# Encoder layer: the first stage rebuilt around column halves of x and pairs of weight units

## The reference, cut to what matters

```python
def rmsnorm(x, w):
    y = xf * lax.rsqrt(jnp.mean(xf * xf, axis=-1, keepdims=True) + EPS)
    return (y * w)
def swiglu(x, w_gate, w_up, w_down):
    return (silu(x @ w_gate) * (x @ w_up)) @ w_down
```

## Time and profile before

| what | value |
| --- | --- |
| median of three runs | 1214.18 us (1213.52 to 1215.35) |
| span of the profiled execution | 1213.9 us |
| TensorE matmul busy | 1125.2 us, 93% of the span |
| VectorE, ScalarE, GpSimd busy | 586.6, 319.1 and 460.9 us |
| mean granted TensorE clock | 0.953 |
| first matmul of the first feed-forward, start | 26.33 us |
| first matmul of unit 4, start | 52.73 us |

### The profile page before, as it was taken

One profiled execution on the slowest core, in us unless ns is written; L12 is line 12 of the kernel. 1 busy time (PEld: TensorE's weight loads), 2 busy tenths in 40 slices (PEclk: granted clock), 3 DMA queues, 4 the chain that ended last, 5 costly groups with the idle time before them and its releaser, 6 DMA issues.

```text
span 1213.9 us, 13708 instructions
## 1 busy us (share of the span) xinstructions
PE 1125.2 (93%) x5167; PEld 912.8 (75%) x5167; DVE 586.6 (48%) x774; ACT 319.1 (26%) x458; POOL 460.9 (38%) x211
## 2 busy tenths in 40 slices
PE   4999999999999799898899699879999999999996
PEld 3788888888887578787788356757888888888884
DVE  5584455441000747575664654546754455520004
ACT  4322222222222332111111643334222222222211
POOL 4554444444444542131222220255544444444420
PEclk9999999999999789898899788988999999999996
DMA  7133333323332422121112000130433333233301
GB/s 213 43 115 103 88 102 91 99 88 94 96 95 61 155 87 70 36 53 36 52 36 69 18 1 1 35 104 21 119 99 91 102 88 103 80 96 96 95 15 69
DMA packets 173628, 94.51 MB, mean 78 GB/s; under 512 B 11477, under 2 KB 169753, under 8 KB 173465
## 3 DMA queue, kind: packets, MB, share of 16 engines
q1 hardware_dynamic: 173168, 93.93, 26.2%
q10 hardware_dynamic: 424, 0.10, 0.0%
HBM read 91.92 MB, written 2.10 MB: 77 GB/s over the span
## 4 chain that ended last, share of the span: by engine, by line
PE 85%; DVE 9%; issue 2%; POOL 2%; ACT 1%; DMA 1%; SPq 0%; DVEq 0%; POOLq 0%; ACTq 0%
PE ps L612 23%; PE ps L613 23%; PE ps L614 23%; PE ps L745 4%; PE ps L853 2%; PE ps L709 1%; PE ps L710 1%; PE ps L711 1%; PE ps L783 1%; DVE xT L979 1%; PE ps L868 1%; POOL SSX L354 1%; DMA raw<-ffn_w_gate 1%; PE ps L816 1%; DVE TMP L978 1%
## 5 line engine op out<-in xcount | busy, mean ns | idle before, releaser
L341 POOL TENSOR_TENSOR WL<-raw,WH 128x1024 fp32r<-128x1024 f32 x168 | 407.1, 2426 | 682.6 <-ACT WH L402 682.6
L612 PE MATMUL ps<-XH,WH 128*128 128x512 f32 x912 | 369.1, 405 | 18.3 <-DVE XL L958 8.3
L613 PE MATMUL ps<-XL,WH 128*128 128x512 f32 x912 | 361.9, 397 | 0.0
L614 PE MATMUL ps<-XH,WL 128*128 128x512 f32 x912 | 361.0, 396 | 0.0
L402 ACT ACTIVATE WH<-raw 128x1024 fp32r<-128x1024 f32 (+1 forms) x170 | 176.1, 1038 | 594.5 <-PE ps L614 551.7
L612 PEld LDWEIGHTS ps<-XH,WH 128*128 128x128 f32 x912 | 175.0, 192 | 58.8 <-DVE XL L958 10.6
L614 PEld LDWEIGHTS ps<-XH,WL 128*128 128x128 f32 x912 | 174.4, 191 | 40.4
L613 PEld LDWEIGHTS ps<-XL,WH 128*128 128x128 f32 x912 | 175.1, 192 | 35.6
L612 PE MATMUL ps<-hh,WH 128*128 128x512 f32 x352 | 138.3, 393 | 0.0
L613 PE MATMUL ps<-hl,WH 128*128 128x512 f32 x352 | 137.6, 391 | 0.0
L614 PE MATMUL ps<-hh,WL 128*128 128x512 f32 x352 | 137.3, 390 | 0.0
(11 more groups left out here) (146 smaller groups left out, 937.4 us busy)
## 6 DMA issues: line engine op xcount, KB each, us to landing
raw<-ffn_w_gate SPq DMA_DIRECT2D x44, 512.0 KB, 3.8
raw<-ffn_w_up SPq DMA_DIRECT2D x44, 512.0 KB, 3.8
raw<-ffn_w_down SPq DMA_DIRECT2D x32, 448.0 KB, 3.3
raw<-w_in SPq DMA_DIRECT2D x22, 512.0 KB, 3.8
raw<-ffn_w_down SPq DMA_DIRECT2D x16, 512.0 KB, 3.6
raw<-w_out SPq DMA_DIRECT2D x8, 512.0 KB, 3.5
xin<-x SPq DMA_DIRECT2D x4, 512.0 KB, 5.5
raw<-w_in SPq DMA_DIRECT2D x8, 256.0 KB, 3.4
```

The source lines that it names most:

```text
L341: pool.tensor_tensor(WL[:, s, 0:size], raw[:, s, 0:size], WH[:, s, 0:size].bitcast(fp32), ALU.subtract).then_inc(lo_done, 3 if n == 2 else 1)
L612: nc.tensor.matmul(dst, WH[:, s, w], xh, start=first, stop=False)
L613: nc.tensor.matmul(dst, WH[:, s, w], xl, start=False, stop=False)
L614: return nc.tensor.matmul(dst, WL[:, s, w], xh, start=False, stop=last)
```

## The change

- x is loaded in halves by channel. The first half (channels 0 to 511 of all tokens, two transfers) comes before units 0 and 1, the second half between units 1 and 2. Each half has one semaphore.
- The first norm's weights have a semaphore of their own (`pre_in`), are transposed first, and are copied to `g0`.
- There are four `turn` banks. k = 0 to 3 are transposed at the start; k = 4 to 7 inside the first pair of units, after k = 1, 2, 3 and 4. Each of these waits until the bank's old block was copied to `xT`.
- XH and XL are made from the `turn` bank in PSUM, not from `xT`, which is now copied four blocks later (the last four after all low parts).
- Units 0 and 1 are multiplied first, through all k, then units 2 and 3. Between them TensorE waits for the copies of all of x and for the small loads, and transposes the small loads.
- The squares are taken by ScalarE along the rows of the untransposed x, with the row sum as an accumulated output; eight such sums (two halves by four token blocks) replace squares, GpSimd's sums and `stat`. `spread` comes after k = 3 of the second pair.
- ScalarE makes the high parts of units 0 to 3 between those of x (after k = 1, 2, 4, 5). Its sqrt is no longer preloaded: the order is sqrt, exp, sigmoid.

```diff
+        g0, ssx = sb("g0", [P, KD]), sb("ssx", [P, 3, TT])
...
-        turn = (ps[4], ps[5], ps[7])
+        turn = (ps[4], ps[5], ps[2], ps[3])
...
-        const_in, mix_in, x_in = sem("const_in"), sem("mix_in"), [sem(f"x_in{c}") for c in range(TT)]
-        CONST_IN, MIX_IN = 11 * 16, 4 * 16
+        const_in, mix_in, x_in = sem("const_in"), sem("mix_in"), [sem(f"x_in{h}") for h in range(2)]
+        CONST_IN, MIX_IN = 10 * 16, 4 * 16
...
+            def load_x(half):
+
+                f = slice(half * (D // 2), (half + 1) * (D // 2))
+                for c in range(0, TT, 2):
+                    src = io["x"][0, c * P:(c + 2) * P, f].rearrange("(c p) d -> p c d", p=P)
+                    sp.dma_start(xin[:, c:c + 2, f], src).then_inc(x_in[half], 16)
...
                 for b in range(NSLOT):
                     load(first + b, 0, (gate, up)[b % 2][:, :, (b // 2) * P:(b // 2 + 1) * P])
+                    if s == 1 and b == 1:
+                        load_x(1)
...
             sp.dma_start(ident[:, :], io["t_square"][:, 0:P]).then_inc(ident_in, 16)
-            for c in range(TT):
-                sp.dma_start(xin[:, c, :], io["x"][0, c * P:(c + 1) * P, :]).then_inc(x_in[c], 16)
+            load_x(0)
             load_ffn(1, FFN1)
...
                     lo(first + b, 0, SLOT)
-                sum_x(e)
+                if e:
...
-                act.wait_ge(stat_ready, s + 1)
-                nc.scalar.activation(rt_root[:, s, :], STAT[:, 0:TT], ACT.Sqrt, bias=eps[:, :], scale=1.0 / D).then_inc(root_ready, 1)
+                if s:
+                    act.wait_ge(stat_ready, s)
+                else:
+                    act.wait_ge(rows_summed, 1)
+                nc.scalar.activation(rt_root[:, s, :], STAT[:, 0:TT] if s else ssx[:, 2, :], ACT.Sqrt, bias=eps[:, :], scale=1.0 / D).then_inc(root_ready, 1)
...
+                if not e:
+                    if not k:
+                        act.wait_ge(pre_ready, 1)
+                    act.wait_ge(x_turned, k + 1)
+                    nc.scalar.activation(XH[:, k, :], turn[k % 4][:, :], ACT.Copy, scale=g0[:, k:k + 1]).then_inc(xh_ready, 1)
+                    return
...
+            def square_rows(half):
+
+                for c in range(TT):
+                    n = TT * half + c
+                    if n >= 2:
+                        act.wait_ge(rows_squared, n - 1)
+                    nc.scalar.activation(SQX[:, n % 2, :], xin[:, c, half * TOK:(half + 1) * TOK], ACT.Square,
+                                         accum_out=ssx[:, half, c:c + 1]).then_inc(rows_squared, 1)
+
             def ffn(f, first):
-                for k in range(KD):
-                    split_high(2 * f, k)
+                if f:
+                    for k in range(KD):
+                        split_high(2, k)
+                else:
+                    for k in range(KD):
+                        split_high(0, k)
+                        if k in (1, 2, 4, 5):
+                            ahead((1, 2, 4, 5).index(k))
+                        if k == 3:
+                            square_rows(0)
+                    square_rows(1)
+                    root(0)
                 if not f:
-
                     act.wait_ge(lb_max, 1)
                     nc.scalar.activation(lbr, lbr, ACT.Exp).then_inc(lb_exp, 1)
-                    preload(ACT.Sqrt)
-                root(4 * f)
+                else:
+                    root(4)
                 preload(ACT.Sigmoid)
...
             for name in ("ffn1_pre_norm", "ffn1_post_norm", "mix_pre_norm", "mix_post_norm", "ffn2_pre_norm", "ffn2_post_norm"):
-                act.dma_start(vec_rows[row:row + KD, :], io[name][0].rearrange("(k p) -> k p", p=P)).then_inc(const_in, 16)
+                act.dma_start(vec_rows[row:row + KD, :], io[name][0].rearrange("(k p) -> k p", p=P)).then_inc(const_in if row else pre_in, 16)
                 row += KD
...
             act.dma_start(HGN[:, :], io["hgrn_out_norm"][0].partition_broadcast(P)).then_inc(const_in, 16)
-            ahead(3)
             act.wait_ge(set_up, 1)
             ffn(0, FFN1)
...
                 for k in range(KD):
                     pe.wait_ge(xl_ready, KD * e + k + 1)
                     pe.wait_ge(xh_ready, KD * e + k + 1)
-                    if k == KD - (1 if e else 2):
-                        stat(2 * e, SSX, x_summed, KD * e + KD)
-                    if k == KD - 1 and not e:
-                        spread(0)
+                    if k == KD - 1 and e:
+                        stat(2 * e, SSX, x_summed, KD * e)
...
                         mm = three(bank[:, :], (first + u) % NSLOT, k, XH[:, k, :], XL[:, k, :], not k, k == KD - 1)
                         if k == KD - 1:
                             mm.then_inc(unit_used, 1)
+                    if not e and not first and 0 < k < 5:
+                        turn_x(k + 3)
+                    if not e and first and k == 3:
+                        spread(0)
...
             def ffn(f, first):
-                abreast(first, ps[0:4], 2 * f)
+                if f:
+                    abreast(first, ps[0:4], 2)
+                else:
+                    abreast(first, ps[0:2], 0)
+                    pe.wait_ge(x_ready, KD)
+                    pe.wait_ge(const_in, CONST_IN)
+                    pe.wait_ge(pre_ready, 1)
+                    nc.tensor.transpose(ps[6][:, 0:NV], vec_rows[:, :], ident[0:NV, 0:NV]).then_inc(vecs_turned, 1)
+                    abreast(first + 2, ps[2:4], 0)
                 with pe.Fori(0, KF // 2 - 1) as i:
                     for a in range(2):
...
+            def turn_x(k):
+
+                if k >= 4:
+                    pe.wait_ge(x_ready, k - 3)
+                for c in range(TT):
+                    if k % 4 == 0:
+                        pe.wait_ge(x_in[k // 4], 32)
+                    mm = nc.tensor.transpose(turn[k % 4][:, c * P:(c + 1) * P], xin[:, c, k * P:(k + 1) * P], ident[:, :])
+                mm.then_inc(x_turned, 1)
+
             pe.wait_ge(ident_in, 16)
-            for k in range(KD):
-                if k == 3:
-                    pe.wait_ge(const_in, CONST_IN)
-                    nc.tensor.transpose(ps[6][:, 0:NV], vec_rows[:, :], ident[0:NV, 0:NV]).then_inc(vecs_turned, 1)
-                if k >= 3:
-                    pe.wait_ge(x_ready, k - 2)
-                for c in range(TT):
-                    if not k:
-                        pe.wait_ge(x_in[c], 16)
-                    mm = nc.tensor.transpose(turn[k % 3][:, c * P:(c + 1) * P], xin[:, c, k * P:(k + 1) * P], ident[:, :])
-                mm.then_inc(x_turned, 1)
+            pe.wait_ge(pre_in, 16)
+            nc.tensor.transpose(ps[6][:, 0:KD], vec_rows[0:KD, :], ident[0:KD, 0:KD]).then_inc(pre_turned, 1)
+            for k in range(4):
+                turn_x(k)
             ffn(0, FFN1)
...
                 dve.wait_ge(xh_ready, KD * e + k + 1)
+                if not e:
+                    nc.vector.scalar_tensor_tensor(out=XL[:, k, :], in0=turn[k % 4][:, :], scalar=g0[:, k:k + 1],
+                                                   in1=XH[:, k, :].bitcast(fp32), op0=ALU.mult, op1=ALU.subtract).then_inc(xl_ready, 1)
+                    return
...
             def take_rms(e):
-                inverse(2 * e)
+                if e:
+                    inverse(2 * e)
...
-            def take_x(k):
-                dve.wait_ge(x_turned, k + 1)
-                nc.vector.tensor_copy(xT[:, k, :], turn[k % 3][:, :]).then_inc(x_ready, 1)
-
-            for k in range(3):
-                take_x(k)
-            for u in range(2):
-
-                dve.wait_ge(hi_done, u + 1)
-                nc.vector.tensor_tensor(WL[:, u, :], raw[:, u, :], WH[:, u, :].bitcast(fp32), ALU.subtract).then_inc(lo_first, 1)
+            nc.vector.memset(small[:, 32:33], 0.0).then_inc(set_up, 1)
+            dve.wait_ge(pre_turned, 1)
+            nc.vector.tensor_copy(g0[:, :], ps[6][:, 0:KD]).then_inc(pre_ready, 1)
+            dve.wait_ge(pre_ready, 1)
+            for k in range(KD + 4):
+                if k >= 4:
+                    nc.vector.tensor_copy(xT[:, k - 4, :], turn[k % 4][:, :]).then_inc(x_ready, 1)
+                if k in (2, 3):
+                    dve.wait_ge(hi_done, k - 1)
+                    nc.vector.tensor_tensor(WL[:, k - 2, :], raw[:, k - 2, :], WH[:, k - 2, :].bitcast(fp32),
+                                            ALU.subtract).then_inc(lo_first, 1)
+                if k < KD:
+                    dve.wait_ge(x_turned, k + 1)
+                    split_low(0, k)
+            dve.wait_ge(rows_squared, 2 * TT)
+            nc.vector.tensor_tensor(ssx[:, 2, :], ssx[:, 0, :], ssx[:, 1, :], ALU.add).then_inc(rows_summed, 1)
+            inverse(0)
...
-            dve.wait_ge(const_in, CONST_IN)
-            nc.vector.memset(small[:, 32:33], 0.0).then_inc(set_up, 1)
-            for k in range(KD):
-                if k >= 3:
-                    take_x(k)
```

(24 more changed lines are left out.)

## The result

The changed kernel takes 1223.87 us (median of 5 runs, 1222.88 to 1229.33) against 1214.18 (5 runs): 1.008 times as long, 95% interval 1.0055 to 1.0104. It is 9.7 us slower. I had forecast 8.1 us faster.

The account below looks back on a forecast made before the run. TensorE, 85% of the chain, was taken as the bound. Unit 4 at 44.5 instead of 52.73 us gave -8.2; with 0.1 added for rounding, the median 1214.18 becomes 1206.1 us, range 1203.0 to 1210.3.

Parts of the forecast that it names:

- The step that failed: From unit 4 on, the chain is back-to-back matmuls; starting its first one earlier shortens the run equally, here 8.2 us.
- Second pair: Units 2 and 3: 48 matmuls at 0.229 (11.0 us) plus `spread` 0.80, from 32.7, so unit 4 begins at 44.5.
- the ring: Transposes of k = 4 to 7 wait for `turn` copies: 3.32 us a turn, TensorE idle about 1.05 three times.
- the tail of the pair with the join: End of units 0 and 1: copies and matmuls from 27.3 to 32.3, then 0.4 for transposing the vectors.
- Half of x: First-stage load: half of x, the bytes of two old blocks, there at 6.4 us, 6.5 with shorter pieces.
- The table load stays in the wait: ScalarE's start: the table load at 5.26 us stays inside the wait for x, so it delays nothing.
- Weights come two blocks earlier: Loads of units 0 and 1 move up 3.3 us; high parts possible from 9.2 and 11.1, not 12.53 and 14.36.
- rival 1: Weights of units 0 and 1 land no earlier than now: +3.3 us, 1209.4; chance 12%.
- Two speeds: TensorE's matmuls: six, one k of a pair, cost 1.37 us at the high clock and 2.58 at the low.
- Rival 4: TensorE's clock stays low after starting in small portions: unit 4 at about 58.4, +5.7 us, 1219.9, slower; chance 3%.
- Rival 5: Gain given back: the norm slips and unit 4 or 6 waits, or later clock falls worsen: 1213; chance 3%.
- rival 2: The ring is longer, with two low parts running beside it (XL over 0.9 us): +2.4 us; chance 14%.

Follow-up runs that it names:

- e1: The changed kernel with g0 and ssx as free columns of `small`, so later tensors keep their old addresses; 1206.8 us, ratio 0.9933 to the kernel before.
- g4: e1 with 448 unused bytes ahead of `sink`, moving XH, XL and the hidden values; 1191.8 us, ratio 0.9805.
- g3: e1 with the copies to `xT` moved up, each later one directly behind its own low part; 1202.8 us.
- e2: The kernel before with an unused tensor of 96 bytes per partition ahead of `sink`, no instruction changed; 1233.0 us, ratio 1.014.
- g6: The kernel before with 192 unused bytes ahead of `sink`, no instruction changed; 1202.9 us, ratio 0.9896.
- f1b: Second run of the kernel before with 96 unused bytes ahead of `xT`, moving all tensors alike; 1215.5 us, ratio 0.9998.

## Why the prediction was wrong

**The step that failed** is in the first paragraph: "whatever brings that matmul forward shortens the whole run by as much, as long as nothing behind it is fed later", with 0.229 us for every matmul. I took the matmul's cost as the chip's and checked only what feeds it. Of the part "Loads" to "Second pair" none mentions the line that adds two tensors; it was costed at nothing without a word. It cost 5.4 ns on each of the 3072 split matmuls of the feed-forwards behind unit 4, 16.6 us (17.0 measured). The span lost 15.4 between unit 4 and the end, since the mixer gave 1.6 back. In medians it is 17.1 against e1 (1223.9 and 1206.8), and 19.2 when each is set against the kernel before beside it (9.7 slower and 9.5 faster). The same paragraph takes the chain behind unit 4 for matmuls alone, though VectorE holds 9% of the whole chain: in the mixer the time doesn't simply move with the start.

**The mechanism of the first stage was right, its sum partly by luck.** e1 measures the change without the shift: 1206.8 us against a forecast of 1206.1. But errors in the terms cancel: transpose 4 started 2.1 us late (19.39, not 17.3), three turns of the ring caught up 1.4 of it, and the tail of the pair with the join took 4.8 us instead of 5.4. Term by term, on the trace after:

Timelines of ScalarE, VectorE, GpSimd and SyncE in the changed kernel, 0 to 75 us:

```profile
9.09 1.28 ACT L451 ACT_TABLE_LOAD   x1 [9.09 <-PE ps L743]
...
11.54 1.05 ACT L414 ACTIVATE WH<-raw 128x1024 fp32r<-128x1024 f32 x1
...
13.05 1.06 ACT L414 ACTIVATE WH<-raw 128x1024 fp32r<-128x1024 f32 x1
...
20.03 0.69 ACT L451 ACTIVATE XH<-ps,g 128x512 fp32r<-128x512 f32 x1 [2.90 <-PE ps L743]
```

```profile
20.82 0.75 DVE L1010 SCALAR_TENSOR_TENSOR XL<-ps,g,XH 128x512 fp32r<-128x512 f32 x1 [3.92 <-ACT XH L451]
21.49 0.68 DVE L1097 COPY xT<-ps 128x512 f32<-128x512 f32 x1
23.71 0.75 DVE L1010 SCALAR_TENSOR_TENSOR XL<-ps,g,XH 128x512 fp32r<-128x512 f32 x1 [1.54 <-ACT XH L451]
...
29.49 0.75 DVE L1010 SCALAR_TENSOR_TENSOR XL<-ps,g,XH 128x512 fp32r<-128x512 f32 x1 [1.54 <-ACT XH L451]
```

```profile
21.80 2.39 POOL L352 TENSOR_TENSOR WL<-raw,WH 128x1024 fp32r<-128x1024 f32 x1 [21.35 <-ACT WH L414]
```

```profile
3.31 4.84 SPq L298 DMA_DIRECT2D xin<-x  x2
```

- *Half of x* is used at 7.86, not 6.5. I had no row for the shorter pieces. The page's median from issue to landing is 6.4 us for the four transfers of x, where it was 5.5; why was not looked into.
- *The table load stays in the wait*: wrong. It runs from 9.09, after the wait for the first transpose, and puts 1.28 us on the way to XH0. In the old kernel it stood ahead of the wait for the first weights. In kernel.py the old first operation stands behind one wait (`raw_full`), the new one behind three (`set_up`, `pre_ready`, `x_turned`). In all eight kernels run with the new order the load stands behind the wait, from 8.60 (g4) to 9.28 us (g3); why it does isn't shown. With x late as well, unit 0 began at 14.00, not 11.7.
- *Weights come two blocks earlier*: right in effect. The high parts of units 0 and 1 start at 11.54 and 13.05 directly behind XH, so rival 1 didn't occur. SyncE, though, was held for 4.84 us in its issue of the second half of x, which I had at 0.9. No transpose waited for that half. (The old kernel's issue of the third unit, in the same place, took 5.18.)
- *Two speeds.* The first three matmuls at 14.00 ran at the high level (0.23 us from 14.31 to 14.54), the seven from 15.70 on at the low one, at 0.43. The two costs in the sum are those of before: 0.43 from 27.33 to 27.76, and 0.229 over 67 distances from 28.37 to 43.71; six matmuls make 2.58 and 1.37. Stretches of the changed kernel, with the granted clock third from the end:

```profile
7.80:11.90 4.10, 3.68 (x16) 3.28 (x16) 0.69 (x2) 2.80 (x4) 0.00 (x0) 1.00 1.14 315
11.90:15.33 3.43, 0.94 (x3) 0.49 (x3) 3.43 (x5) 3.43 (x7) 0.00 (x0) 1.00 1.13 332
15.33:18.74 3.41, 3.04 (x7) 2.49 (x8) 1.57 (x3) 1.80 (x6) 0.00 (x0) 0.54 0.45 111
18.74:32.70 13.96, 11.46 (x55) 8.43 (x55) 7.26 (x12) 7.94 (x15) 4.76 (x2) 0.99 0.57 147
```

The 1.00 of the first row is no reading: the trace's first record of the clock starts at 12.2 us. In before the first starts at 28.06, and a stretch ahead of it reads 1.00 as well, although a matmul cost 0.43 in it:

```profile
26.30:28.10 1.80, 1.80 (x6) 1.50 (x5) 1.64 (x3) 1.36 (x3) 1.66 (x2) 1.00 1.20 290
```

By their times the transposes from 7.86 were at the low level: sixteen in 3.68 us are 0.92 for four. Four took 0.77 to the next start in e2 from 25.65, where the granted clock was 0.50, and 0.36 here from 19.39, where it was 1.00. From 12.2 the record is high (1.00), from 15.6 low (0.50), from 19.0 high again, and the ring, with pauses of 0.83 us, kept it. The fall at 15.6 came behind 3.43 us with 0.94 busy; the ring's pauses show no such fall, and what brings one about isn't shown. The fall cost seven matmuls 0.2 us each here, not the run. Where the clock first rises differs from run to run with the same instructions on TensorE: the first record, 1.00 in each, starts at 12.2 us here, at 10.95 in e1 and at 20.19 in g3. Here are the sixteen transposes and the first matmuls of g3, all of them still low:

```profile
8.05 3.68 PE L743 MATMUL ps<-ident,xin 128*128 128x128 f32 x16 [4.98 <-DMA xin<-x]
14.19 0.77 PE L650 MATMUL ps<-XH,WH 128*128 128x512 f32 x1 [2.46 <-DVE WL L1101]
14.75 0.63 PE L651 MATMUL ps<-XL,WH 128*128 128x512 f32 x1
15.18 0.63 PE L652 MATMUL ps<-XH,WL 128*128 128x512 f32 x1
```

Rival 4 had the right sign of the result for the wrong reason: from 19 us to the end of the first down projection no split matmul was at 0.43. Rival 5's later falls of the clock went the other way: the low clock between 390 and 900 us was 10 us shorter than before.
- *The ring* took 2.84 to 2.89 us a turn, not 3.32, with 0.83 idle instead of 1.05: four transposes at the high clock last 0.66, not 1.12, and displace about 0.4 us of matmuls, not 0.9. This paid back most of the late start: the second pair began at 32.79 (32.7). XL took 0.75 at 23.71, partly beside GpSimd's low part of 21.80 to 24.19, and 0.75 at 29.49 with GpSimd idle, so rival 2 fell: no run shows the +2.4 that the range takes for it, and all four turns had XL at 0.75.
- *Second pair* 12.2 us instead of 11.8: 48 x 5.4 ns, the shift again, and some 0.1.

None of the rivals named the place of operands. A range for it could not have come from the trace of before, in which the distance has one remainder only. But the line was in the diff.

## What to carry to other kernels

A small tensor added ahead of others moves everything behind it (here by 96 bytes). In a kernel whose span is nearly all matmuls, compare the addresses of their operands before and after an edit, and compare the matmul's start-to-start time before reading anything else; if it moved, undo the move first. Here a remainder of 0 by 256 bytes between weights and moving operand was the best of seven. A pad alone (12.8 us in g6, 8.1 of it by faster matmuls) was worth at least as much as the rebuilt stage (9.5 in e1, 8.5 of it by unit 4).

## What the runs showed of the hardware

- The start-to-start time of back-to-back matmuls (128 x 128 fp32r weights, 512 columns, high clock) depends on the distance in SBUF between the weights and the moving operand: 0.2267 to 0.2343 us, 3.4%, over the seven remainders by 256 that were run. Moving both by the same 96 bytes changed nothing (f1b). At a remainder of 0 every start-to-start time of g6 from 100 to 230 us is 226 or 227 ns; at 64 (before) they run from 225 to 232, at 160 (after) from 230 to 239. In this stream (before) each weight load starts 2 to 4 ns after the start of a matmul and lasts 0.188 us. Why the distance in SBUF counts isn't shown.
- At a remainder of 64 one execution had 0.2333 through its second feed-forward, others 0.2289. The kernel before, at this remainder, spread from 1212.4 to 1218.9 us in one set of 13 runs; whether that is the same effect was not looked at (4.4 ns on the 1584 matmuls of one feed-forward would be 7.0).
- Transposes alone can be followed by the high clock. In e1 the record is high from 10.95 us, inside the sixteen transposes: the last two start 0.117 us apart, those before them 0.213, and all took 3.43 us instead of 3.68. But they needn't be: in g3 the same sixteen took 3.68 and the matmuls from 14.19 to 19.47 were low. Nor must they stand in a row: in e2, with the old spread transposes, the record is high from 13.5 us and its last twelve took 2.35 us, where before they took 2.77.
